# Modulation sums moved from VectorE to GpSimd in slabs, the rest cut into quarters, and weight loads put behind the gathers: a two-block transformer kernel on one core

## The reference

```python
for l in range(2):
    mod = silu(c) @ ada_w[l] + ada_b[l]              # 1024 x 6144, one row c
    sh1, sc1, g1, sh2, sc2, g2 = split(mod, 6)
    xm = rms_norm(x) * (1 + sc1) + sh1
    q, k, v, u_pool, ga, gp = split(xm @ w_in[l])
    attn = gqa(rope(norm(q)), rope(norm(k)), v) @ w_attn_o[l]
    pool = multiscale_pool(u_pool) @ w_pool_o[l]
    merged = sigmoid(ga) * attn + sigmoid(gp) * pool
    x = x + g1 * (merged @ w_out[l])
    xf = rms_norm(x) * (1 + sc2) + sh2
    s = (xf @ w_query[l]) . sub_keys[l]              # 8 heads, two halves
    eidx, g = product_key_top16(s)                   # 16 of 16384 experts per head
    act = gelu(xf . expert_u[l][eidx]) * g           # gathered rows
    x = x + g2 * sum(act * expert_v[l][eidx])        # gathered rows
```

## Time and profile before

| what | us |
|---|---|
| median of 3 runs | 3324.11 (3322.91 to 3329.79) |
| the profiled execution, its own time | 3305.74 |
| its span | 3303.9 |
| attention out to first gather, layer 0 / layer 1 (layer's last attention transposes copied, to GpSimd L2722) | 81.1 / 75.1 |
| experts, layer 0 / layer 1 | 781.9 / 778.7 |
| second block and what follows the last expert sum | 1254.9 |

### The profile page before, as it was taken

How to read it: one execution, slowest core, us unless ns; L and a number is a source line. 1 busy time by engine, 2 the same in 40 slices (tenths; PEclk the granted TensorE clock), 3 DMA queues, 4 the chain that set the end, 5 groups by cost and what they waited for, 6 DMA issues and landing times.

```text
span 3303.9 us, 34806 instructions
## 1 busy us (share of the span) xinstructions
PE 2436.2 (74%) x12607; PEld 1736.3 (53%) x12607; DVE 2090.4 (63%) x4416; ACT 933.8 (28%) x1486; POOL 1044.1 (32%) x1060
## 2 busy tenths in 40 slices
PE   5996555545435987664455544999999999999998
PEld 4854422212101855442122210779878987987797
DVE  7868576666655957576666654665555555556654
ACT  2511011101101521011011101554554445445543
POOL 0105566666663204556666664000010001000000
PEclk9998777666666998776677665989999999999999
DMA  9858999999998847899999998435543543554253
GB/s 351 291 194 314 345 377 380 356 386 359 342 371 327 296 175 266 330 362 394 368 377 360 363 371 328 163 103 194 187 140 141 180 159 107 178 188 170 103 192 126
DMA packets 307809, 884.99 MB, mean 268 GB/s; under 512 B 22376, under 2 KB 31568, under 8 KB 307536
## 3 DMA queue, kind: packets, MB, share of 16 engines
q0 software_dynamic: 147456, 536.94, 42.4%
q1 hardware_dynamic: 160208, 346.20, 29.6%
HBM read 882.00 MB, written 1.05 MB: 267 GB/s over the span
## 4 chain that ended last, share of the span: by engine, by line
PE 55%; issue 13%; DVE 10%; POOL 9%; another core or an unknown queue 7%; DMA 3%; ACT 2%; SPq 1%; DVEq 0%; PEld 0%; POOLq 0%; ACTq 0%
PE lin L810 8%; PE lin L812 8%; PE lin L811 8%; POOL proj L2722 4%; PE psS L1069 4%; PE lin L1111 4%; PE lin L986 3%; DVE proj L2391 3%; POOL vbuf L2735 2%; POOL ring L2735 2%; PE psS L1031 2%; PE psT L812 2%; PE psT L811 2%; PE psS L811 2%
## 5 line engine op out<-in xcount | busy, mean ns | idle before, releaser
L2391 DVE CUSTOM_DVE_ANT_0 proj<-proj,psT 128x1024 f32<-128x1024 f32 x512 | 606.6, 1219 | 213.8 <-DMA proj<-in_expert_u,eidx 143.3
L1886 DVE TENSOR_TENSOR weights_split<-ring,weights_split 128x1024 fp32r<-128x1024 f32 (+1 forms) x360 | 431.6, 1207 | 376.1 <-ACT weights_split L1670 373.5
L2722 POOL DMA_INDIRECT proj<-in_expert_u,eidx x512 | 481.4, 940 | 448.8 <-DVEq L2367 241.6
L1670 ACT ACTIVATE weights_split<-ring 128x1024 fp32r<-128x1024 f32 (+1 forms) x376 | 391.5, 1046 | 467.7 <-PE lin L812 291.6
L1111 PE MATMUL lin<-vbuf,rowb 128*32 128x512 f32 x1024 | 255.0, 876 | 279.8 <-issue 162.9
L2758 POOL TENSOR_TENSOR weights_split<-ring,weights_split 128x1024 fp32r<-128x1024 f32 x16 | 37.9, 2379 | 998.2 <-ACT weights_split L1670 998.2
L810 PE MATMUL lin<-weights_split,xT_high 128*128 128x512 f32 (+1 forms) x736 | 294.3, 400 | 16.8 <-issue 8.1
L2735 POOL DMA_INDIRECT ring<-in_expert_v,pT x224 | 211.7, 945 | 242.9 <-remote 94.5
L812 PE MATMUL lin<-weights_split,xT_high 128*128 128x512 f32 (+1 forms) x736 | 287.6, 391 | 0.0
L1111 PE MATMUL lin<-ring,rowb 128*32 128x512 f32 x896 | 193.7, 766 | 125.0 <-issue 62.2
L2735 POOL DMA_INDIRECT vbuf<-in_expert_v,pT x256 | 241.2, 942 | 112.2 <-issue 74.4
(11 more groups left out here) (323 smaller groups left out, 4969.9 us busy)
## 6 DMA issues: line engine op xcount, KB each, us to landing
ring<-in_mlp_w_up SPq DMA_DIRECT2D x32, 2048.0 KB, 8.0
ring<-in_mlp_w_down SPq DMA_DIRECT2D x32, 2048.0 KB, 7.8
ring<-in_w_in SPq DMA_DIRECT2D x16, 2048.0 KB, 12.1
ring<-in_w_query SPq DMA_DIRECT2D x14, 2048.0 KB
vbuf<-in_ada_w SPq DMA_DIRECT2D x12, 2048.0 KB, 11.6
ring<-in_diff_w_in SPq DMA_DIRECT2D x12, 2048.0 KB, 7.9
proj<-in_ada_w SPq DMA_DIRECT2D x16, 1024.0 KB, 5.2
ring<-in_moba_w_in SPq DMA_DIRECT2D x6, 2048.0 KB, 7.9
```

Of the source, the lines that this page charges most:

```text
L1670: act.activation(part(p, 0, kind, w), raw_piece(slot, p, kind, w), ACT.Copy).then_inc(hi_ready, 1)
L1886: dve.tensor_tensor(part(p, 1, kind, w), raw_piece(slot, p, kind, w), part(p, 0, kind, w).bitcast(F32), ALU.subtract).then_inc(lo_ready, 1)
L2391: dve.tensor_tensor_reduce(ubuf[:, n % GB, :], ubuf[:, n % GB, :], x_row, 1.0, 0.0, ALU.mult, ALU.add, hdot[:, cb, k:k + 1]).then_inc(h_re ...
L2722: pool.indirect_dma_start(out=ubuf[:, (16 * c + k) % GB, :], out_offset=None, in_=table["u"], in_offset=bass.IndirectOffsetOnAxis(ap=eidx[ ...
```

## The change

**Next layer's mixing sums.** In layer 0, mix 0 to 3 become 32 slabs of 128x512 (256 KB). SyncE loads them into four buffers in the q columns of `proj` (L661 of the changed kernel). GpSimd scales each by its column of c (L2745 for a unit's first, L2748 for the other seven) and adds it (L2735) into `mix_acc`, two places in the memory of the causal and band masks, which are loaded again after layer 1. All 32 slabs stand in GpSimd's queue ahead of its first gather. TensorE's `mix_sum(0)` stands ahead of the attention product of tile 0, `mix_sum(1)` behind `W_out`'s two products, `mix_sum(2)` and `mix_sum(3)` behind tile 0's scores; GpSimd's slab 16 waits for the first, slab 24 for the second, by the semaphore `mix_done`.

**Last two units in quarters.** ada 10 and 11 are loaded and summed in eight quarters of two pieces (512 KB, two buffers). VectorE has quarters 0 to 5 ahead of tile 0's gates, 6 and 7 behind `gated(0, 1)`.

**Tile 1 in tile 0's gaps.** Its attention product is cut into pieces (`second_tile_attn`), of which k = 0 (k = 0 and 1 in layer 1) stands ahead of the normed rows' transposes, k up to 4 behind them, and 5 to 7 behind tile 0's scores. All of tile 1's gates and `merged` stand behind `topk_part(0, 3)`; its two remaining pooling and attention products too. On ScalarE one query copy of tile 1 stands a chunk later.

**First weights late.** The next stage's first unit is loaded in four quarters with four semaphores, and only once all v sets have landed; the masks and the final norm's row follow it. Seven more semaphores are cleared at a layer's end.

```diff
-        late_at = [proj[:, t, 0:4 * UC].rearrange("p (k n) -> p k n", n=UC) for t in range(2)]
+        late_at = [proj[:, t, 2 * UC:4 * UC].rearrange("p (k n) -> p k n", n=UC) for t in range(2)]
+        slab_at = [proj[:, i % 2, (i // 2) * UC:(i // 2 + 1) * UC] for i in range(4)]
+        mix_acc = [cst("causal"), cst("band")]
...
+            def first_unit(w):
+                for p in range(NPC):
+                    sp.dma_start(ring[:, 0, 2 * p:2 * p + 2, :], cols_of(w, 0, UC)[:, 2 * p:2 * p + 2, :]).then_inc(in0_ld[p], 16)
...
+                def late_quarter(j):
+                    if j >= 2:
+                        sp.wait_ge(late_read, j - 1)
+                    k = 2 * (j % 4)
+                    sp.dma_start(late_at[j % 2], cols_of(T["ada_w"][l], (10 + j // 4) * UC, UC)[:, k:k + 2, :]).then_inc(late_ld[j % 2], 16)
+                def slabs(lo, hi):
+                    for i in range(lo, hi) if l + 1 < DEPTH else []:
+                        if i >= 4:
+                            sp.wait_ge(mix_step, i - 3)
+                        sp.dma_start(slab_at[i % 4], cols_of(T["ada_w"][l + 1], (i // KC) * UC, UC)[:, i % KC, :]).then_inc(slab_ld[i % 4], 16)
...
+                sp.wait_ge(tr_used, 4 + 5)
+                slabs(0, 14)
                 sp.wait_ge(pv_done, GQA.nout)
-                late_half(0, 0)
-                late_half(0, 1)
+                late_quarter(0)
+                late_quarter(1)
...
+                for j in range(2, QUARTERS):
+                    late_quarter(j)
+                    slabs(10 + 2 * j, 12 + 2 * j)
+                slabs(26, SLABS)
...
+                for s in range(NSET):
+                    sp.wait_ge(v_ld[s], (l + 1) * VLANDED)
+                first_unit(T["w_in"][l + 1] if l + 1 < DEPTH else T["diff_w_in_2"][0])
...
+                if later:
+                    mix_sum(0)
...
+                def second_tile_attn(k0, k1):
+                    for k in range(k0, k1):
+                        mm = pe.matmul(lin[:, 2, :], xT[:, k, P:2 * P], ring[:, 0, k, :], start=(k == 0), stop=(k == KC - 1))
+                    if k1 == KC:
+                        C.lin += 1
+                        mm.then_inc(lin_done, 1)
...
-                half_linear(1, 0, xT, KC, out_columns(1), beside_out)
+                half_linear(1, 0, xT, KC, out_columns(1))
+                pe.wait_ge(sk_used, 1)
+                ada_sum(10)
+                if later:
+                    mix_sum(1)
                 pe.wait_ge(lin_used, lin0 + 3)
-                half_linear(2, 1, xT, KC, ring[:, 0, :, :], beside_attn)
+                second_tile_attn(0, 1 if later else 2)
+                pe.wait_ge(gates_read, 1)
+                ada_sum(11)
                 normed_rows(0, lambda g: psT[:, g, :])
-                pe.wait_ge(lin_used, lin0 + 4)
-                half_linear(3, 1, mixT, 4, poolw[:, :, 0:UC])
+                second_tile_attn(1 if later else 2, 5)
                 pe.wait_ge(q0_ld, 16)
-                pe.wait_ge(sk_used, 1)
+                pe.wait_ge(gates_read, 2)
                 pe.wait_ge(tr_used, C.tr)
                 tile_query(0, 0)
-                if later:
-                    mix_sum(2)
                 pe.wait_ge(lin_used, lin0 + 6)
                 rows_back(0)
                 tile_scores(0, 0)
-                pe.wait_ge(lin_used, lin0 + 7)
-                half_linear(2, 1, mixT, 4, poolw[:, :, UC:2 * UC])
+                second_tile_attn(5, KC)
+                pe.wait_ge(lin_used, lin0 + 4)
+                half_linear(3, 1, mixT, 4, poolw[:, :, 0:UC])
+                pe.wait_ge(tr_used, C.tr)
+                half_linear(0, 1, mixT, 4, poolw[:, :, UC:2 * UC])
                 if later:
+                    mix_sum(2)
                     mix_sum(3)
-                pe.wait_ge(lin_used, lin0 + 8)
-                half_linear(3, 1, xT, KC, ring[:, 1, :, :])
+                half_linear(1, 1, xT, KC, ring[:, 1, :, :])
...
+            def late_quarter(j):
+                q = SUM_AT["ada", 10 + j // 4]
+                acc = ada_acc[:, q % 2, :]
+                dve.wait_ge(late_ld[j % 2], 16 * (j // 2 + 1))
+                if j % 4 == 0:
+                    dve.wait_ge(s_ada, q - 1)
+                for b in range(2):
+                    k, w = 2 * (j % 4) + b, late_at[j % 2][:, b, :]
+                    if k == 0:
+                        ins = dve.tensor_scalar(acc, w, cact[:, 0:1], None, ALU.mult)
+                    else:
+                        ins = dve.scalar_tensor_tensor(out=acc, in0=w, scalar=cact[:, k:k + 1], in1=acc, op0=ALU.mult, op1=ALU.add)
+                    link(ins)
+                dve.sem_inc(late_read, 1)
+                if j % 4 == 3:
+                    dve.sem_inc(acc_ready, 1)
...
-                late_unit(l, 0)
-                late_unit(l, 1, 0)
+                for j in range(6):
+                    late_quarter(j)
...
-                gate_row(1, 0, psS[:, 1, :])
-                late_unit(l, 1, 1)
+                late_quarter(6)
+                late_quarter(7)
                 pool_gated(0, 0, 2)
                 merged(0, 0)
-                if later:
-                    late_unit(l, 2, 0)
+                row_columns(0, 0, psT_bank)
                 pool_gated(0, 1, 3)
                 merged(0, 1)
-                row_columns(0, psT_bank)
+                row_columns(0, 1, psT_bank)
+                residual_row(0, 0)
+                residual_row(0, 1)
+                gate_row(1, 0, psS[:, 1, :])
+                dve.sem_inc(gates_read, 1)
+                norm_row(0)
                 gate_row(1, 1, psS[:, 1, :])
                 dve.sem_inc(gates_read, 1)
-                if later:
-                    late_unit(l, 2, 1)
-                    late_unit(l, 3, 0)
-                residual_row(0, 0)
-                if later:
-                    late_unit(l, 3, 1)
-                residual_row(0, 1)
-                norm_row(0)
-                gated(1, 0, 2)
                 scaled_columns(0, psT_bank)
-                pool_gated(1, 0, 3)
-                merged(1, 0)
-                if later:
-                    late_unit(l, 4)
-                    late_unit(l, 5)
                 rows_back(0)
...
+                for step in range(4):
+                    topk_part(0, step)
+                gated(1, 0, 2)
+                pool_gated(1, 0, 3)
+                merged(1, 0)
+                pool_gated(1, 1, 0)
+                gated(1, 1, 1)
...
+                def slab_added(i):
+                    n = i // KC
+                    pool.wait_ge(mix_scaled, i - n)
+                    pool.wait_ge(mix_step, i)
+                    pool.tensor_tensor(mix_acc[n % 2], slab_at[i % 4], mix_acc[n % 2], ALU.add).then_inc(mix_step, 1)
+                for i in range(SLABS) if l + 1 < DEPTH else []:
+                    n, k = i // KC, i % KC
+                    if k == 0:
+                        if n >= 1:
+                            slab_added(i - 1)
+                        if n >= 2:
+                            pool.wait_ge(mix_done, n - 1)
+                        pool.wait_ge(slab_ld[i % 4], 16 * (i // 4 + 1))
+                        pool.tensor_scalar(mix_acc[n % 2], slab_at[i % 4], cact[:, 0:1], None, ALU.mult).then_inc(mix_step, 1)
+                    else:
+                        pool.wait_ge(slab_ld[i % 4], 16 * (i // 4 + 1))
+                        pool.tensor_scalar(slab_at[i % 4], slab_at[i % 4], cact[:, k:k + 1], None, ALU.mult).then_inc(mix_scaled, 1)
+                        if k > 1:
+                            slab_added(i - 1)
+                if l + 1 < DEPTH:
+                    slab_added(SLABS - 1)
```

119 lines of the change are left out of this document (42 added, 77 removed).

## The result

The changed kernel takes 3350.43 us, median of 16 runs (3340.27 to 3369.17), against 3323.76 for the kernel before in as many runs beside it (3315.18 to 3334.21): a ratio of 1.0089, 95% interval 1.0071 to 1.0107. It is slower, by 26.7 us between the medians; the forecast was 3314, in the range of 3297 to 3333. The profiled execution took 3349.98 us, span 3348.2, mean granted clock 0.83.

The account below looks back on a forecast made before the run. It took the transitions as bound by a chain through the engines, the experts by DMA bytes. Terms -6.3 + 7 - 5 - 6 + 0.5 = -9.8 took 3324.1 to 3314 us, range 3297 to 3333.

Parts of the forecast that it names:

- The slab's price: GpSimd, layer 0: scaling 0.7 plus add 1.25, a slab 1.95 us, bounds 1.6 and 3.0.
- the twentieth add: Layer 0: done at 211.3, releasing SyncE's last quarter; `merged` then at 220.5, first gather at 270.3, +7.
- Held ports: Rival: GpSimd and VectorE hold each other; at 3.0 us a slab layer 0 is 25 us later, time 3332; chance 0.17.
- cheap slabs: Rival: at 1.6 us a slab layer 0's first gather comes at 259.6, -4, time 3303; chance 0.20.
- `mix_sum(0)`: TensorE, layer 0: slabs ready at 179.9, so it starts some 5 us late, which does not bind.
- Tile 1 at zero: Expert phases: first gathers cover tile 1's late gates and `merged`; 0, bounds -2 and +3 a layer.
- The ends: Layer ends: late weights let last gathers land sooner; -5.0 in layer 0, -6 in layer 1.
- the clearing itself: Layer ends: seven more semaphores to clear, twice, cost +0.5 in all.
- The final norm's row: End of layer 1: the row lands some 10 us after the last gather, behind 2.6 MB; 1 us is lost.
- late weights give nothing: Rival: last gathers are bound by issue, not bytes, so both ends stay; time 3325, chance 0.18.
- Layer 1's transition: Attention out to first gather, without slabs: `merged` at +20.9, gather at +68.7 against +75.1, -6.3.

Follow-up runs that it names:

- e4: Changed kernel with six instead of fourteen slabs loaded ahead of the quarters and `mix_sum(0)` behind tile 0's attention product; ratio 1.0003 to the kernel before.
- second pair: Kernel before and changed kernel, both traced again on one other chip; spans 3176.8 and 3203.4 us, ratio 1.0061.
- e10: Changed kernel with slabs reordered, two-input scaling, tile 1's old order, first weights behind clearing, masks earlier, query weights behind sixth quarter; ratio 1.0007 to before.
- e9: Changed kernel with tile 1's product, gates and `merged` where they stood before the change; ratio 1.0074 to the kernel before.
- first pair: The first profiled executions of the kernel before and the changed kernel; spans 3303.9 and 3348.2 us.
- e3_weights_early: Changed kernel without the wait for the v sets, so next weights go out amid the last gathers; ratio 1.0113 to the kernel before.
- e1_no_slabs: Changed kernel without slab loads, scalings and adds, `mix_sum` summing a constant; ratio 0.9988 to the kernel before.

## Why the prediction was wrong

**The slab's price was the term that failed.** "The scaling has one input", said the prediction, and "I take 0.7, nearer to the small end, since the add reads two". It measured 1.56, more than the two-input add (1.26 against 1.25 forecast). The reason for the choice, one input against two, does not hold for these forms; the forecast's slab of 1.95 was 2.79. The bounds (up to 3.0) held it. The steps that hang on it came out as told, at that price: the twentieth add was forecast at 164.3 + 20 x 1.95 + 8 of waits = 211.3. With 2.79, the start at 165.75 and the measured wait of 9.2 it is 165.75 + 55.8 + 9.2 = 230.8, and SyncE is past slab 23 at 230.44. The last quarter then took 4.4 us to its sums (forecast 4.3), `merged` ended at 239.8 and the gather went out at 287.7. So 19.3 us were lost by `merged`, forecast at 220.5, and 1.9 won back behind it. The mechanism, late quarters that hang on slabs through SyncE's queue, is shown by *e4*: another order at the same price moves the gather to 269.8.

The Trainium skill (GPSIMD Engine Reference, 3.1 Elementwise, side-by-side cycle accounting) has 769 ns for a one-input loop over 512 elements, as the best case of a tight loop, half of the 1.56 us measured. It was to make the time 3316; the measurement decides.

**Held ports** named the number, 25 us at 3.0 a slab against 24.2 measured (20.4 in the second pair), but not the cause: the base price makes 2.79, and GpSimd is held only in single operations (1.61 and 2.0 at most, medians 1.262 and 1.562). The number was luck in part: by the prediction's own steps 3.0 a slab puts the gather at 235.5 + 49.8 = 285.3, which is +22 (49.8 being 44.3, 3.5 and 2), and the 288 it gave is worked out nowhere. The same steps give 260.3 and not 259.6 for cheap slabs, and -6.4 and not -6.3 for layer 1. For VectorE the holds are real: its pairs take 1.85 to 2.86 us in layer 0's transition and 1.54 in layer 1's. In the changed kernel most of that hides behind the waits for quarters; the last pair (2.86) and `merged` (1.14 against 0.69) put 1.8 us on the path. In *e10* the holds bind. The rule of the Trainium skill on the shared pair (SBUF — State Buffer, SBUF: two separate sides), an exclusive lock, can go with this, but no run here tells a lock from a pair that is shared otherwise. The one-input scaling is held too (0.94 against 0.49); the rule covers it only if it ran in a two-port mode, which no run here tells.

**`mix_sum(0)`** was to start 5 us late and not to bind: it came with a wait of 11.93, and TensorE's later wait of 26.84 swallows it. Right in kind, and too short for the same reason: the eighth slab was added at 186.9, where 179.9 was forecast.

**Tile 1 at zero** failed: "The experts' first gathers cover it", at zero with +3 a layer as the bound. The pieces do fit the gaps of the transition, but the fifth gather waits for tile 1's gates, the second chunk's query product comes later, and +5.0 and +3.7 were measured on one chip (*e9* takes them back). The first pair of traces shows +12.5 and +13.1, of which the second chunk explains 9.8 and 3.4, and 5.5 of the 9.8 are the late copy that stays open. The rest is not explained; with the same order of tile 1, layer 1's phase took 771.0 us in *e3_weights_early* and 766.8 in *e1_no_slabs*, against 764.7 and 766.4 before, so most of the 13.1 does not come back.

**The ends** gave -2.8 and -2.2 (-2.8 and -3.1 on the other chip) for a forecast of -5.0 and -6. The landing was right: 6.53 us for 12.07. What was left out are SyncE's own loads, 1.9 and 3.4 us of issue ahead of the clearing; the clearing itself got 0.7 longer at each end, where 0.5 was forecast for both together. Taken off the 5.5 and 6.3 us (7.57 for 13.90 in layer 1) that the gathers land sooner, these leave 2.8 and 2.2. The final norm's row, however, was there in time: its use, which waits for ScalarE's `st` and not for a DMA, came 21.3 us behind the last gather, against 23.5 before:

```profile
2101.80 2.60 DVE L1856 SCALAR_TENSOR_TENSOR x_res<-x_res,st,tokb 128x1024 f32<-128x1024 f32 x2 [0.33 <-ACT st L1488]
```

Neither layer end was a loss, and "late weights give nothing" falls.

**Layer 1's transition** came out as forecast: -6.3 forecast, -6.0 measured, `merged` at +22.1 (20.9), from there to the gather 47.0 (47.8), two small misses against each other. The length was right, 69.1 and 69.0 us for 68.7. That the gain was right too is luck: the other two traces of the kernel before have 72.0 and 71.9 and not 75.1, and against these it is -2.9.

Put together: +24 (+20 in the second pair) for +7, +9 to +26 for 0 in the experts, -5 to -6 for -11 at the ends, +4 to +5 in layer 1's projections, where nothing was forecast. These projections take 144.6, 148.7 and 145.0 us in the three traces of the kernel before; the granted clock in the 10 us behind the first product is 1.00, 0.70 and 1.00 there, and 0.70 and 0.69 in the two traces of the changed kernel, so these 4 us are the clock's and not shown to be the change's. The median moved by 26.7 us, with held ports' sign and beyond its 3332.

## What to carry to other kernels

Work that is moved to an idle engine takes its place in the queues that feed it. Ask first what stands behind its loads, and put what the critical chain reads ahead of it: here the order was worth 19 us, a third off the scaling's price 7. Take the price of the exact form of instruction on the exact engine; where no row has it, let the bound that the design can't stand decide the chance. And if work behind a search is pushed out of a transition, see who reads what it writes, for it may only be lent by the next stage.

Of the parts of this change only the late loads were shown to be worth having, in a simpler form: next weights issued behind the clearing of semaphores, 0.2 to 0.3% faster than the kernel before. The quarters cost 2.7 us where they stand alone.

## What the runs showed of the hardware

- On GpSimd a 128x512 float32 multiply by a column took 1.56 us as TENSOR_SCALAR and 1.04 us as TENSOR_TENSOR with the column broadcast (medians of 28 each); an add of two tensors took 1.26.
- While both work, GpSimd and VectorE stretch each other: VectorE's pair of sums 1.54 to as much as 2.97 us, its one-input scaling 0.49 to 0.94, GpSimd's add 1.26 to 1.61.
- SyncE took 1.91 us to issue four loads of 512 KB in a row, about 0.48 each, and that is time on the path where a clearing stands behind.
- Chips differ in the pace of indirect gathers: the kernel before took 763 to 770 us from first to last gather of a layer in two traces and 692 to 694 in a third, from another chip, while the rest behind the experts took 1250 to 1253 us in all three. The last gather landed later behind its issue there (20.9 and 23.9 us against 11.5 to 14.6), so to the last landing it is 774 to 782 against 715 to 716.
- On one chip a copy started 15 us behind the last record of its matmul, while gathers were in flight, and on another, with the same kernel, it did not. Four traces with the slower gathers show it, at 5.5 to 15.2 us, and none with the faster. This is open.
- TensorE's granted clock in the first 10 us of layer 1's products was 1.00 in two traces of the kernel before and 0.70 in the third, and the stage took 4 us longer with 0.70.
